# An fp32 decoder trunk on one core: expert weights loaded as whole row blocks, the experts' up products with k outside in five banks, their down products in four column groups, 64-column mixer products in halves

## What is computed

```python
def swiglu(h, w1, w3, w2):
    return (jax.nn.silu(h @ w1) * (h @ w3)) @ w2

def moe_swiglu(h, router, w1, w3, w2):
    logits = (h @ router).astype(F32)
    top_vals, top_idx = lax.top_k(logits, TOP_K)
    gates = jax.nn.softmax(top_vals, axis=-1)
    combine = jnp.sum(jax.nn.one_hot(top_idx, N_EXPERTS, dtype=F32) * gates[..., None], axis=-2)
    out = jnp.zeros_like(h)
    for e in range(N_EXPERTS):
        out = out + combine[..., e:e + 1].astype(h.dtype) * swiglu(h, w1[e], w3[e], w2[e])
    return out
```

## Time and profile before

| | |
|---|---|
| three timed runs | 1139.45, 1142.22 (median), 1143.24 us |
| profiled execution, its own time | 1143.13 us |
| its span | 1141.3 us |
| TensorE matmul busy (PE) | 1102.5 us, 97% |
| VectorE, ScalarE, GpSimd busy | 25%, 17%, 5% |
| one turn of the expert loop | 55.1 us, eight turns |

### The profile page before, as it was taken

How to read it: one execution, slowest core, us unless ns; L and a number is a source line. 1 busy time by engine, 2 the same in 40 slices (tenths; PEclk the granted TensorE clock), 3 DMA queues, 4 the chain that set the end, 5 groups by cost and what they waited for, 6 DMA issues and landing times.

```text
span 1141.3 us, 22432 instructions
## 1 busy us (share of the span) xinstructions
PE 1102.5 (97%) x9790; PEld 837.2 (73%) x9790; DVE 285.3 (25%) x645; ACT 192.9 (17%) x444; POOL 61.4 (5%) x67
## 2 busy tenths in 40 slices
PE   8999999899999999999999969999999999999996
PEld 6887887488888543887789549595949494949592
DVE  4432473500000001233376341020111112021112
ACT  2244231100000001214323011011010111101011
POOL 2000411000000000000312100000000000000000
PEclk8999999999999999999999989999999999999998
DMA  9633101335554445343210256989898989899870
GB/s 325 196 122 105 43 1 38 111 117 160 160 159 167 156 148 155 119 135 109 74 38 1 74 185 203 343 279 351 287 344 289 343 293 323 305 301 332 279 272 37
DMA packets 168650, 213.34 MB, mean 187 GB/s; under 512 B 5120, under 2 KB 151200, under 8 KB 168480
## 3 DMA queue, kind: packets, MB, share of 16 engines
q1 hardware_dynamic: 166032, 210.29, 56.0%
q10 hardware_dynamic: 2576, 2.45, 0.7%
HBM read 211.67 MB, written 1.05 MB: 186 GB/s over the span
## 4 chain that ended last, share of the span: by engine, by line
PE 95%; DVE 3%; issue 1%; ACT 1%; POOL 0%; DMA 0%; DVEq 0%; POOLq 0%; ACTq 0%
PE bank L518 93%; PE bank L523 1%; DVE tok L1434 1%; POOL small L1343 0%; DMA x_sb<-in_x 0%; DVE b_att L1616 0%; DVE b_q L1413 0%; PE bank L1045 0%; DVE x_sb L1410 0%; PE bank L829 0%; ACT tok L1121 0%; DVE small L1425 0%; ACT hT L1133 0%; DVE hT L1410 0%; PE bank L797 0%
## 5 line engine op out<-in xcount | busy, mean ns | idle before, releaser
L518 PE MATMUL bank<-hT,ring 128*128 128x256 f32 (+1 forms) x1184 | 260.3, 382 | 0.0
L518 PEld LDWEIGHTS bank<-hT,ring 128*128 128x128 f32 (+1 forms) x1184 | 223.4, 189 | 36.1 <-issue 2.7
L518 PEld LDWEIGHTS bank<-region_m,ring 128*64 128x64 f32 x4096 | 170.3, 137 | 8.6 <-issue 8.6
L518 PE MATMUL bank<-region_m,ring 128*64 128x96 f32 x4096 | 173.7, 246 | 2.9 <-DVE region_m L1860 1.6
L518 PE MATMUL bank<-ring,region_e 128*96 128x512 f32 (+1 forms) x368 | 160.0, 594 | 0.0
L518 PEld LDWEIGHTS bank<-ring,region_e 128*96 128x96 f32 (+1 forms) x368 | 64.1, 176 | 89.5 <-issue 88.5
L518 PE MATMUL bank<-ring,hT 128*128 128x256 f32 (+1 forms) x448 | 127.8, 442 | 1.4 <-ACT hT L1138 1.4
L518 PE MATMUL bank<-region_e 128*128 128x128 f32 (+2 forms) x512 | 119.2, 384 | 0.0
L1410 DVE TENSOR_TENSOR region_e<-region_f,bank 128x96 f32<-128x96 f32 (+1 forms) x110 | 31.7, 288 | 341.7 <-ACT region_f L1318 198.9
L518 PEld LDWEIGHTS bank<-ring,hT 128*128 128x128 f32 x448 | 84.0, 190 | 35.7 <-issue 25.8
L518 PEld LDWEIGHTS bank<-region_e 128*128 128x128 f32 (+1 forms) x512 | 71.9, 191 | 46.9 <-issue 46.8
(11 more groups left out here) (234 smaller groups left out, 715.0 us busy)
## 6 DMA issues: line engine op xcount, KB each, us to landing
ring<-in_moe_w SPq DMA_DIRECT2D x80, 1024.0 KB, 6.9
region_e<-in_moe_w SPq DMA_DIRECT2D x40, 1024.0 KB, 6.8
ring<-in_ffn_w SPq DMA_DIRECT2D x33, 1024.0 KB, 5.4
ring<-in_w_in SPq DMA_DIRECT2D x22, 1024.0 KB, 5.4
ring<-in_w_out SPq DMA_DIRECT2D x8, 1024.0 KB, 4.9
ring<-in_moe_w SPq DMA_DIRECT2D x16, 512.0 KB, 5.8
region_e<-in_moe_w SPq DMA_DIRECT2D x8, 512.0 KB, 4.0
ring<-in_w_in SPq DMA_DIRECT2D x2, 1088.0 KB, 5.5
```

Of the source, the lines that this page charges most:

```text
L518: return nc.tensor.matmul(o, lhsT, rhs, start=start, stop=stop, skip_group_check=True)
```

## The change

All large SBUF tiles become parts of one tile `arena`, so that the experts' buffers can be laid out anew: `rows_a` holds sixteen row blocks (w1 and w3, each whole rows of 1408 floats, 5,632 bytes in one run), `rows_b` the eleven of w2: a whole expert, loaded in sixteen and six loads. Space for the first expert's loads comes free as the ring's last pieces are used and when x is updated after the mixers.

The up products run with k outside: for each k the eleven w1 tiles (banks 0, 1 and the first 96 columns of bank 4), then the eleven w3 tiles (bank 4, 2, 3), each still in two halves of 64 weight columns. `moe_row_used` frees two row blocks after each k. Silu and multiply then work on five chunks (480 columns) at once.

The down products are cut into 32 weight columns (`QUARTER`) by 256 moving columns. A round (`down_round`) is four matmuls, one in each group of 32 output partitions; three rounds make one k. The last three k are done round by round, so that bank 5 is complete before bank 6 is. `slot_y` is put together by five copies, and the scatter goes to banks 1 to 4, the low half of y first.

The mixers' products with 64 moving columns, the bonus product (`BON`, 2 columns) and the router's (8 columns) are issued in two halves of 64 weight columns (`mm_halves`).

```diff
+ROWS_A = 2 * KC
+ROWS_B = 6
...
-    for name, bank in (("RT", 6), ("POS", 7), ("G0", 6), ("G1", 7)):
+    for name, bank in (("RT", 6), ("POS", 7), ("G0", 7), ("G1", 0)):
...
+a_landed = [ctx.enter_context(nc.semaphore(f"row_a{k}_landed")) for k in range(ROWS_A)]
+b_landed = [ctx.enter_context(nc.semaphore(f"row_b{k}_landed")) for k in range(ROWS_B)]
+GATE = [(0, j * CAP) if j < 5 else (1, (j - 5) * CAP) if j < 10 else (4, 0) for j in range(UPC)]
+UP = [(2, j * CAP) if j < 5 else (3, (j - 5) * CAP) if j < 10 else (4, CAP) for j in range(UPC)]
+per = [2, 2, 2, 2, 2, 2, 1, 1]
...
+    def expert_row_a(e, k):
+        w = t_in["moe_w1" if k % 2 == 0 else "moe_w3"]
+        sp.dma_start(rows_a[:, k, :], w[0, e, (k // 2) * P:(k // 2 + 1) * P, :]).then_inc(a_landed[k], 16)
+    def expert_rows_b(e, b):
+        m = min(2, UPC - 2 * b)
+        src = t_in["moe_w2"][0, e].rearrange("(c p) n -> p c n", p=P)[:, 2 * b:2 * b + m, :]
+        sp.dma_start(rows_b[:, 2 * b:2 * b + m, :], src).then_inc(b_landed[b], 16)
...
+    for k in range(ROWS_A):
+        first, last = k * D_FFE // SLOT, ((k + 1) * D_FFE - 1) // SLOT
+        if last < SLOTS:
+            for r in range(first, last + 1):
+                wait_released(max(n for n in range(FIRST_MOE) if slot(n) == r))
         else:
...
-        elif k == SLOTS:
             sp.wait_ge(sem("x_updated"), 2 * NT * (2 * (DEPTH - 1) + 1))
+        expert_row_a(0, k)
+    for b in range(ROWS_B):
+        expert_rows_b(0, b)
...
+        for k in range(ROWS_A):
+            if k < ROWS_A - 2:
+                sp.wait_ge(sem("moe_row_used"), i * (KC - 1) + k // 2 + 1)
+            else:
+                sp.wait_ge(full[3], nth(i, 3, 1))
+            expert_row_a((i + 1) % N_EXPERTS, k)
+        for b in range(ROWS_B):
+            if b < ROWS_B - TAIL:
+                sp.wait_ge(sem("moe_w2_used"), i * (ROWS_B - TAIL) + b + 1)
+            else:
+                sp.wait_ge(full[6], nth(i, 6, 1))
+            expert_rows_b((i + 1) % N_EXPERTS, b)
...
+    def mm_halves(o, lhsT, rhs, start=False, stop=False):
+        for q in range(0, P, HALF):
+            last = mm(o[q:q + HALF, :], lhsT[:, q:q + HALF], rhs, start=start, stop=stop)
+        return last
...
-            mm(o[:, c], a_pt[:, s, :], a_v[:, 0, v], start=(s == 0), stop=True)
+            mm_halves(o[:, c], a_pt[:, s, :], a_v[:, 0, v], start=(s == 0), stop=True)
             c = slice(GW + s * HD, GW + (s + 1) * HD)
-            mm(o[:, c], a_pt[:, 4 + s, :], a_v[:, 0, v])
-            last = mm(o[:, c], a_pt[:, 8 + s, :], a_v[:, 1, v], stop=True)
+            mm_halves(o[:, c], a_pt[:, 4 + s, :], a_v[:, 0, v])
+            last = mm_halves(o[:, c], a_pt[:, 8 + s, :], a_v[:, 1, v], stop=True)
...
+        def up_tile(place, k, row, j, start):
+            b, at = place
+            return mm_halves(banks[b][:, at:at + CAP], rows_a[:, row, j * P:(j + 1) * P], slot_h[:, k, :],
+                             start=start, stop=(k == KC - 1))
+        def down_round(k, r):
+            for g in range(4):
+                a, c = (g, r) if g < 3 else (r, 3)
+                o = banks[5 + r // 2][g * QUARTER:(g + 1) * QUARTER, (r % 2) * GW:(r % 2 + 1) * GW]
+                last = mm(o, slot_act[:, k, a * QUARTER:(a + 1) * QUARTER], rows_b[:, k, c * GW:(c + 1) * GW],
+                          start=(k == 0 and r != 1), stop=(k == UPC - 1))
+            return last
...
         with pe.Fori(0, n_passes * N_EXPERTS) as i:
+            pe.wait_ge(free[7], nth(i, 7, 0))
+            pe.wait_ge(free[0], nth(i, 0, 0))
+            for k in range(KC):
+                pe.wait_ge(a_landed[2 * k], 16 * i + 16)
+                for j in range(5):
+                    last = up_tile(GATE[j], k, 2 * k, j, k == 0 and j == 0)
+                if k == KC - 1:
+                    last.then_inc(full[0], 1)
+                if k == 0:
+                    pe.wait_ge(free[1], nth(i, 1, 0))
+                for j in range(5, 10):
+                    last = up_tile(GATE[j], k, 2 * k, j, k == 0 and j == 5)
+                if k == KC - 1:
+                    last.then_inc(full[1], 1)
+                if k == 0:
+                    pe.wait_ge(free[4], nth(i, 4, 0))
+                up_tile(GATE[10], k, 2 * k, 10, k == 0)
+                pe.wait_ge(a_landed[2 * k + 1], 16 * i + 16)
+                last = up_tile(UP[10], k, 2 * k + 1, 10, False)
+                if k == KC - 1:
+                    last.then_inc(full[4], 1)
+                if k == 0:
+                    pe.wait_ge(free[2], nth(i, 2, 0))
+                for j in range(5):
+                    last = up_tile(UP[j], k, 2 * k + 1, j, k == 0 and j == 0)
+                if k == KC - 1:
+                    last.then_inc(full[2], 1)
+                if k == 0:
+                    pe.wait_ge(free[3], nth(i, 3, 0))
+                for j in range(5, 10):
+                    last = up_tile(UP[j], k, 2 * k + 1, j, k == 0 and j == 5)
+                if k == KC - 1:
+                    last.then_inc(full[3], 1)
+                else:
+                    last.then_inc(sem("moe_row_used"), 1)
+            pe.wait_ge(sem("weighs"), i + 1)
+            pe.wait_ge(free[5], nth(i, 5, 0))
+            for t in range(NT):
+                last = nc.tensor.transpose(banks[5][0:CAP, t * P:(t + 1) * P], weigh[:, t, :], ident)
+            last.then_inc(full[5], 1)
+            pe.wait_ge(sem("picks"), i + 2)
+            gather((nth(i, 7, 0), nth(i, 0, 1)))
+            pe.wait_ge(free[5], nth(i, 5, 1))
             pe.wait_ge(free[6], nth(i, 6, 0))
...
-            for k2 in range(UP2):
-                m = min(2, UPC - 2 * k2)
-                landed_piece(i, 2 * UP2 + k2)
-                w = expert_slot(2 * UP2 + k2, m * D).rearrange("p (c n) -> p c n", c=m)
-                for kk in range(m):
-                    j = 2 * k2 + kk
-                    pe.wait_ge(free[j % 2], nth(i, j % 2, j // 2 + 1))
-                for half in range(2):
-                    for kk in range(m):
-                        k = 2 * k2 + kk
-                        last = mm(banks[2 + half][0:CAP, :], slot_act[:, k, :],
-                                  w[:, kk, half * 512:(half + 1) * 512], start=(k == 0), stop=(k == UPC - 1))
-                    if k2 == UP2 - 1:
-                        last.then_inc(full[2 + half], 1)
-                if k2 < UP2 - 1:
+            for k2 in range(ROWS_B):
+                pe.wait_ge(b_landed[k2], 16 * i + 16)
+                if k2 == 0:
+                    pe.wait_ge(free[2], nth(i, 2, 1))
+                elif k2 == 2:
+                    pe.wait_ge(free[3], nth(i, 3, 1))
+                elif k2 == 5:
+                    pe.wait_ge(free[4], nth(i, 4, 1))
+                if k2 < ROWS_B - TAIL:
+                    for k in (2 * k2, 2 * k2 + 1):
+                        for r in range(3):
+                            last = down_round(k, r)
                     last.then_inc(sem("moe_w2_used"), 1)
-            for q, (b, t, half) in enumerate(SCATTER):
-                pe.wait_ge(free[2 + half], nth(i, 2 + half, 2 - half))
-                if b > 3:
-                    pe.wait_ge(free[b], nth(i, b, 0))
+            for r in range(3):
+                for k in range(2 * (ROWS_B - TAIL), UPC):
+                    last = down_round(k, r)
+                if r:
+                    last.then_inc(full[4 + r], 1)
+            for b, t, half in SCATTER:
+                if half == 0:
+                    pe.wait_ge(sem("moe_y_low"), i + 1)
+                else:
+                    pe.wait_ge(sem("moe_y_high"), 2 * i + 2)
+                pe.wait_ge(free[b], nth(i, b, 1))
                 mm(banks[b][:, :], weigh_t[:, t, :], slot_y[:, half * 512:(half + 1) * 512],
                    start=True, stop=True).then_inc(full[b], 1)
...
+                for b in (0, 1):
+                    act.wait_ge(full[b], nth(i, b, 1))
+                    nc.scalar.activation(slot_silu[:, 5 * b:5 * b + 5, :],
+                                         banks[b][:, 0:5 * CAP].rearrange("p (c s) -> p c s", c=5),
+                                         ACT.Silu).then_inc(free[b], 1)
...
-                nc.scalar.copy(slot_y[:, 0:512], banks[2][0:CAP, :]).then_inc(free[2], 1)
+                    last = slots_in(c, 7)
+                last.then_inc(free[7], 1)
+                act.wait_ge(full[5], nth(i, 5, 2))
+                nc.scalar.copy(slot_y[:, 0:512], banks[5][0:CAP, :]).then_inc(sem("moe_y_low"), 1)
+                nc.scalar.copy(slot_y[0:QUARTER, 768:1024], banks[5][CAP:P, 0:GW])
+                nc.scalar.copy(slot_y[QUARTER:2 * QUARTER, 768:1024],
+                               banks[5][CAP:P, GW:2 * GW]).then_inc(free[5], 1)
+                act.wait_ge(free[5], nth(i, 5, 2))
+                act.sem_inc(sem("moe_y_high"), 1)
...
+                dve.wait_ge(sem("moe_silu"), i + 1)
+                tt(slot_act[:, 10, :], slot_silu[:, 10, :], banks[4][:, CAP:2 * CAP],
```

(70 more changed lines are left out.)

182 lines of the change are left out of this document (48 added, 134 removed).

## The result

The changed kernel takes 1164.8 us (median of four runs, 1158.2 to 1168.6) against 1142.4 us for the kernel before (four runs, 1139.5 to 1143.2): a ratio of 1.0195, 95% interval 1.0145 to 1.0244. It is 2% slower, where 1096 us and faster were forecast.

What follows compares the result with a forecast made beforehand. TensorE, busy 97% of the span, was taken as the bound. Expert loop 36.0, first-turn wait 1.4 and mixers 8.8 sum to 46.2 us off 1143.1: 1096.9, forecast 1096; terms' bounds 1084 to 1108, range up to 1130.

Steps and rivals of the forecast that it cites:

- Up products: Expert loop: same 352 matmuls a turn; K outside changes banks and weights, not the number of records; cost 0.
- Issue is no limit: Down products: a record each 41 ns is seen, one each 54 ns is needed.
- The idle time at 714.82: First turn: TensorE's 1.37 us wait, taken for the last w1 and w3 pieces landing; 1.4 us gained (0 to 1.4).
- Down products, 4.5 us a turn: Expert loop: four groups side by side, 19.0 to 14.4 us, less 0.15, plus 0.1; eight turns 36.0 us.
- Scatter, 0.1 us: End of a turn: copies of y fit under down products and first scatter products; worth 0.1 us.
- Loads, cost 0: Expert weights: 17.3 MB in a 50.6 us turn needs 342 GB/s, taken as covered; cost 0.
- The rival in which the DMA is the bound: Expert loop: 5.6 KB runs slower, at 316 GB/s a turn stays 54.8 us; 1131 us; chance 0.05.
- the two on the groups: Down products: only two groups at a time, 1212 us, chance 0.09; four overlap in part, 1123 us, chance 0.08.
- Mixers, 8.8 us: Mixers' halved products gain 12, width changes cost 5.4, net 6.6; router 1.3, BON 0.9; together 8.8 us (2 to 18).
- The block Y1: Mixers, a sign to look for: 24 records now taking 2.6 us would take 1.3 to 2.0 us.
- two groups at a time: Down products: strict record order lets only neighbours overlap, 29.0 us, 10 more than now; 1212 us; chance 0.09.
- a reason unseen: Whole kernel: no gain at all for a reason unseen; chance 0.02.

Runs made afterwards that it cites:

- before with start 196: The kernel before, with only TensorE's expert loop placed at instruction 196 of a block of 256: 1187.8 us, ratio 1.0402 to before.
- old down products: The changed kernel with the down products of before (22 matmuls of 96 weight by 512 moving columns a turn), loop not placed: 1198.4 us, ratio 1.0487 to before.

## Why the prediction was wrong

The cause is shown: from the start of the loop alone, with the same products, times move by 45 to 64 us in both directions. The changed kernel has it for two reasons, each of which is enough: the halved mixers shift the loop to a start from which even the old body no longer fits, and the 420 further instructions of its own body (44 records of down products became 264) put it at nine blocks, which no start cures.

By the prediction's own steps:

- **Up products, "I cost it at 0".** The step that failed. It asked what the new order does to banks and weights, and the down products' part said "Issue is no limit", from records that start 41 ns apart. Nowhere does the sum have a term for bringing the instructions in. What stands in its place: 6.31 us of idle time a turn, and 3.2 us more from the lower clock behind it. The latter is what is left: 60.27 - 6.31 - 50.74, where 50.74 is a turn undisturbed, worked out and not measured: 0.35 + 21.20 + 29.19 us, the last of them the up products of the earlier trace rows. 9.5 us in each of seven turns is 67 us.
- **The idle time at 714.82, "I take it for a landing".** Wrong, and it was the clue. It stands where a block ends, with a packet of instructions just moved, and it moves or goes with the loop's start. Of the 1.4 us forecast, none came: the first turn of after, from the loop's start at 681.00 to 713.57, is 1.65 us longer than that of before (689.28 to 720.20), 2.42 us of idle time at block ends in place of 1.37, and 704 up records that take 0.6 us longer in all.
- **Down products, 4.5 us a turn.** Right: 14.77 us against 14.4 + 0.15 forecast. Four groups do run side by side. The Trainium skill's 2.38 times for three column tiles (TensorE: Matmul & The Clock Gate, Part 3) is not borne out here, at fp32: the four are worth four. The undisturbed turn of 50.74 us, 4.34 less than before, stands against 50.6 forecast; the nearest turn measured without idle time is the 51.45 us with 512 moving columns, whose gather at full width takes 3.48 us for 2.80.
- **Scatter, 0.1 us.** It starts right behind the down products and takes 796.57 - 792.87 = 3.70 us for 3.74 before: 0.04, with the last copy of y (793.41, 0.43 us) under its first products.
- **Loads, cost 0.** Right: TensorE waits for no row in the loop; the DMA moves 369 and, a turn later, 340 GB/s during gather, down products and scatter, goes on for some 2 us and then rests for about 10. The rival in which the DMA is the bound is out, as are the two on the groups.
- **Mixers, 8.8 us.** Right: the loop starts 689.28 - 681.00 = 8.3 us earlier, and with the fetch out of the way the kernel with halved mixers is 1133.0 against 1143.6 us, 10.6 us less, of which 1.4 is the idle time of the first turn. The block Y1 takes 1.62 us (x48), inside the 1.3 to 2.0 forecast, and 1.0 less than before for its 12 matmuls; at that rate 144 would give the 12 us that were taken. The router's 32 records of 4.8 us became 64 of 3.6.
- **Chances and range.** None of the cases with a mechanism came in. Of the 0.10 for slower, 0.09 was for two groups at a time; a loss from outside the products had only the 0.02 for "a reason unseen". The bounds of the terms add up to 1084 and 1107, not 1108.

The profiled span adds up: -8.3 (mixers) + 1.65 (first turn) + 36.3 (seven turns at +5.19) - 4.8 (from the last pair of transposes to the end, 30.8 against 35.5 us, a down product saved and no jump behind it) = +24.9 us, and 1166.2 - 1141.3 is 24.9.

The Trainium skill has the rule that the sum lacked (Runtime: NRT & Kernel Launch, Instruction fetch mechanics): instructions come in 16 KiB blocks of 256, TensorE's store holds 128 KiB, and "Branching breaks sequential prefetch", so that a taken branch to a block that is not held must wait for a DMA. The runs agree with the block and with the wait, 3.0 to 5.3 us at the jump. The page also says that only a window of two pages counts; here the measurement decides, and seven blocks stay through all turns (32 packets in the whole run). Eight blocks less one fetched ahead would fit its 128 KiB, which is an argument and not shown.

What stays open: why eight blocks with little of the last touched are fetched in every second turn only; why eight blocks cost 6.4 us a turn in one kernel and 9.4 in another (before with start 196, old down products); and whether the idle time at the jump depends on what the DMA queues carry at that moment. None of these was tried.

## What to carry to other kernels

Before a loop's body is cut into more and smaller instructions, count them on the engine that bounds it and lay them out in blocks of 256 from the loop's real start: seven blocks touched cost nothing here, eight cost 4 to 9 us a turn and nine 8 to 9.5, against the 4.3 us that the finer products saved. An edit far ahead of a loop can move it over that edge, so a surprise in untouched code is to be read from the packets of the instruction queue and from idle times that the profile gives to nothing, at equal distances of 128 matmul records. If the body fits, fix its start; if it doesn't, look for the same work in fewer instructions (512 moving columns instead of 256 gave the same 14.77 us), and name the jump's target ahead if neither can be had.

## What the runs showed of the hardware

- Four column groups of 32 at fp32 run fully side by side: 264 records of 256 columns, or 132 of 512, in 14.77 us, that is 0.224 and 0.448 us for four records together, against 0.220 us for one of 256 columns in a dense stretch.
- A loop of 1687 to 1779 instructions on TensorE that touches seven blocks is fetched once; one that touches eight is fetched in each turn (in every second, with 23 instructions in the last), one of nine in each, with 9 and 10 packets a turn.
- The jump back to a block that isn't held takes 3.0 to 5.3 us, with its target named ahead no time, but then 2.4 to 2.9 us at the end of that block; after it (changed kernel, from 739.25) the granted clock was 0.70, 0.50 and 0.57 in the stretches up to 747.50.
- Sixteen loads of whole rows (5.6 KB runs) and six of two row blocks run at 340 to 369 GB/s over gather, down products and scatter; no row came late.
